# Second attention, heads without bias: the odd heads' weights are turned on VectorE, four weight low halves are made on GpSimd

## The reference

```python
s = jnp.einsum('bqhd,bkhd->bhqk', qb, k).astype(jnp.float32) * scale
s = jnp.where(key_idx[None, :] <= q_idx[:, None], s, NEG_INF)
p = jax.nn.softmax(s, axis=-1).astype(v.dtype)
return jnp.einsum('bhqk,bkhd->bqhd', p, v)
# second_block: a_out from mla_attention, b_out from moba_attention
x = x + jnp.concatenate([a_out, b_out], axis=-1) @ w_out[l]
```

## Time and profile before

| | us |
|---|---|
| median of three runs | 966.04 (965.82 to 966.35) |
| profiled execution | 966.08 |
| its span, first to last instruction | 964.2 |
| TensorE busy | 956.4 |
| VectorE busy | 772.1 |
| ScalarE busy | 500.9 |
| GpSimd busy | 162.5 |
| TensorE's granted clock | 0.999 of 2.4 GHz |

### The profile page before, as it was taken

How to read it: one execution, slowest core, us unless ns; L and a number is a source line. 1 busy time by engine, 2 the same in 40 slices (tenths; PEclk the granted TensorE clock), 3 DMA queues, 4 the chain that set the end, 5 groups by cost and what they waited for, 6 DMA issues and landing times.

```text
span 964.2 us, 12923 instructions
## 1 busy us (share of the span) xinstructions
PE 956.4 (99%) x4468; PEld 786.7 (82%) x4468; DVE 772.1 (80%) x1489; ACT 500.9 (52%) x666; POOL 162.5 (17%) x118
## 2 busy tenths in 40 slices
PE   9999999999999999999999999999999999999997
PEld 6887778888888888888888888888887788888886
DVE  6897997578669799884778987877878878887875
ACT  7545556644463644444765444444648665444442
POOL 3552444310013300000133000000133023000000
PEclk9999999999999999999999999999999999999999
DMA  9865555434455755554566656553654255656531
GB/s 343 269 193 167 165 174 175 150 130 175 175 203 205 240 176 191 202 187 164 172 215 196 213 177 204 187 177 113 223 182 147 88 175 187 206 177 206 184 131 44
DMA packets 98725, 175.67 MB, mean 182 GB/s; under 512 B 5920, under 2 KB 54128, under 8 KB 98672
## 3 DMA queue, kind: packets, MB, share of 16 engines
q1 hardware_dynamic: 97024, 171.53, 53.0%
q0 software_dynamic: 1344, 3.19, 1.2%
q10 hardware_dynamic: 304, 0.27, 0.1%
HBM read 173.91 MB, written 1.05 MB: 181 GB/s over the span
## 4 chain that ended last, share of the span: by engine, by line
PE 93%; DVE 4%; issue 1%; ACT 1%; POOL 1%; DMA 0%; POOLq 0%; ACTq 0%; DVEq 0%
PE bank L519 86%; PE bank L533 2%; DVE relu_T L1755 2%; DVE w_lo L1479 1%; PE bank L578 1%; PE bank L577 1%; PE bank L904 1%; PE bank L589 1%; POOL w_lo L2159 0%; ACT w_hi L1034 0%; PE bank L960 0%; DMA g_rows<-in_g_mix 0%; PE bank L591 0%; PE bank L590 0%; DVE act_f L1740 0%
## 5 line engine op out<-in xcount | busy, mean ns | idle before, releaser
L519 PE MATMUL bank<-w_hi,hA 128*128 128x512 f32 (+1 forms) x1752 | 544.8, 390 | 0.0
L1034 ACT ACTIVATE w_hi<-raw 128x2048 fp32r<-128x2048 f32 (+1 forms) x162 | 305.8, 1893 | 196.7 <-PE bank L519 194.9
L519 PEld LDWEIGHTS bank<-w_hi,hA 128*128 128x128 f32 x1752 | 327.4, 188 | 67.7 <-issue 1.1
L1479 DVE TENSOR_TENSOR w_lo<-raw,w_hi 128x2048 fp32r<-128x2048 f32 (+1 forms) x138 | 308.2, 2254 | 63.1 <-ACT w_hi L1034 58.1
L519 PE MATMUL bank<-w_lo,hA 128*128 128x512 f32 (+1 forms) x876 | 334.3, 388 | 0.0
L519 PEld LDWEIGHTS bank<-w_lo,hA 128*128 128x128 f32 x876 | 164.5, 188 | 33.0
L2159 POOL TENSOR_TENSOR w_lo<-raw,w_hi 128x2048 fp32r<-128x2048 f32 x21 | 96.8, 4609 | 154.5 <-ACT w_hi L1034 121.9
L1848 DVE STREAM_TRANSPOSE act_T<-act_f 32x128 f32<-32x128 f32 x352 | 106.5, 303 | 5.7 <-DVE act_f L1836 0.7
L2145 POOL TENSOR_SCALAR ms<-ss 128x1 f32<-128x1 f32 x15 | 9.8, 654 | 515.9 <-ACT junk L1064 515.6
L519 PE MATMUL bank<-w_hi,fT_hi 128*128 128x512 f32 x232 | 71.5, 389 | 0.0
L519 PE MATMUL bank<-w_hi,fT_lo 128*128 128x512 f32 x232 | 71.4, 389 | 0.0
(11 more groups left out here) (281 smaller groups left out, 906.7 us busy)
## 6 DMA issues: line engine op xcount, KB each, us to landing
raw<-in_w_in SPq DMA_DIRECT2D x74, 512.0 KB, 4.7
raw<-in_w_ff SPq DMA_DIRECT2D x64, 512.0 KB, 4.0
raw<-in_ffn_w_gate SPq DMA_DIRECT2D x44, 512.0 KB, 3.9
raw<-in_ffn_w_up SPq DMA_DIRECT2D x44, 512.0 KB, 4.8
raw<-in_ffn_w_down SPq DMA_DIRECT2D x44, 512.0 KB, 4.0
raw<-in_w_out SPq DMA_DIRECT2D x16, 512.0 KB, 3.8
raw<-in_w_branch_diff SPq DMA_DIRECT2D x8, 512.0 KB, 3.9
raw<-in_w_branch_ret SPq DMA_DIRECT2D x8, 512.0 KB, 3.7
```

Source lines behind the costliest of these rows:

```text
L519: mm = pe.matmul(o, a, w, start=first and t == 0 and m < len(outs), stop=last and t == n - 1 and m >= len(todo) - len(outs))
L1034: act.activation(w_hi[u % HI_SLOTS][:, 0:w], raw[u % RAW_SLOTS][:, 0:w], ACT.Copy).then_inc(hi_ready, 1)
L1479: vec.tensor_tensor(w_lo[u % RAW_SLOTS][:, 0:w], raw[u % RAW_SLOTS][:, 0:w], w_hi[u % HI_SLOTS][:, 0:w].bitcast(f32), ALU.subtract).then_i ...
```

## The change

For kind "l" the odd head of a pair is not transposed on TensorE any more and has no work batch. VectorE, after the logits of the next pair, transposes its normalised weights from `L` straight to `aT[1]` in sixteen instructions of 32 partitions and counts `odd_turned`; TensorE waits for that count ahead of the odd head's weighted sums. VectorE's copy from PSUM goes for these heads. The low halves of o2 + 1, o2 + 2, o2 + 3 and f2 are taken from VectorE and appended to GpSimd's list behind the last gain's load; VectorE waits for f2's before it makes that of f2 + 1. ScalarE's `cat_split` waits for the same two pairs as before, by names in place of batch numbers.

```diff
--- before.py
+++ after.py
@@ -116,7 +116,7 @@
     order += [("cq", 0), ("cq", 1), ("ckv",)]
     for kind in "bl":
         for j in range(BH // 2):
-            order += [(kind + "a", 2 * j), (kind + "a", 2 * j + 1)]
+            order += [(kind + "a", h) for h in range(2 * j, 2 * j + 2) if kind == "b" or h % 2 == 0]
             order += [(kind + "v", j)]
     order += [("ffn2", tb, h) for tb in range(TB) for h in range(2)]
     return {name: n for n, name in enumerate(order)}
@@ -348,7 +348,7 @@
     heads_out = [sem("heads_out0"), sem("heads_out1")]
     k_full = sem("k_full")
     a_turned = sem("a_turned")
-    m_turned = sem("m_turned")
+    m_turned, odd_turned = sem("m_turned"), sem("odd_turned")
     a_ready, cat_hi, cat_ready = sem("a_ready"), sem("cat_hi"), sem("cat_ready")
     vec_step, pool_step = sem("vec_step"), sem("pool_step")
     last_half, half_added, half_squared = sem("last_half"), sem("half_added"), sem("half_squared")
@@ -891,6 +891,8 @@
                     head_scores(kind, h)
             for h in (2 * j, 2 * j + 1):
                 m = SOFT[kind, h]
+                if kind == "l" and h % 2:
+                    continue
                 pe.wait_ge(a_ready, m - 2 * DH + 1)
                 turn((kind + "a", h), [L[:, m % 4, b * P:(b + 1) * P] for b in range(3)])
             beside()
@@ -898,7 +900,10 @@
             b = work(name)
             work_free(WB[name])
             for h in (2 * j, 2 * j + 1):
-                turned((kind + "a", h))
+                if kind == "l" and h % 2:
+                    pe.wait_ge(odd_turned, j + 1)
+                else:
+                    turned((kind + "a", h))
                 v = [mv[:, tb, h * BD:(h + 1) * BD] if kind == "b" else v_tm[:, tb, h, :] for tb in range(TB)]
                 a, y = aT[h % 2], b[h % 2 * BD:(h % 2 + 1) * BD]
                 pe.matmul(y[:, 0:SEQ], v[0], a[:, 0:SEQ], start=True, stop=False, skip_group_check=True)
@@ -1339,8 +1344,7 @@
 
         def cat_split(n):
 
-            b = WB[("l" if n < 2 else "b") + "v", 2 * (n % 2) + 1]
-            for k in (b - 3, b):
+            for k in (WB[("l" if n < 2 else "b") + "v", 2 * (n % 2) + j] for j in range(2)):
                 act.wait_ge(work_out[k % 2], k // 2 + 1)
             act.activation(hA[0][:, 2 * n:2 * n + 2, :], yT[:, 2 * n:2 * n + 2, :], ACT.Copy).then_inc(cat_hi, 1)
 
@@ -2016,6 +2020,15 @@
 
             if not last:
                 next_pair(kind, j + 1)
+            if kind == "l":
+                whole = L[:, SOFT["l", 2 * j + 1] % 4, :].rearrange("p (b j f) -> p b j f", j=4, f=32)
+                there = aT[1][:, :].rearrange("p (b a c) -> p b a c", a=4, c=32)
+                vec.wait_ge(a_ready, SOFT["l", 2 * j + 1] - 2 * DH + 1)
+                for a in range(4):
+                    for k in range(4):
+                        t = vec.transpose(there[32 * k:32 * k + 32, :, a, :], whole[32 * a:32 * a + 32, :, k, :])
+                t.then_inc(odd_turned, 1)
+                return
             n = WB[kind + "a", 2 * j + 1]
             vec.wait_ge(work_done, n + 1)
             vec.tensor_copy(aT[1][:, :], work((kind + "a", 2 * j + 1))[:, 0:384]).then_inc(work_out[n % 2], 1)
@@ -2095,24 +2108,19 @@
         cat_split(3)
         normalize_pair("l", 0)
         pair("l", 0, False)
-        lo(U0["o2"] + 1)
         normalize_pair("l", 1)
         pair_y("l", 0)
         pair("l", 1, False)
-        lo(U0["o2"] + 2)
         normalize_pair("l", 2)
         pair_y("l", 1)
         pair("l", 2, False)
         cat_split(0)
         normalize_pair("l", 3)
         pair_y("l", 2)
-        lo_half(U0["o2"] + 3, 0)
         pair("l", 3, True)
-        lo_half(U0["o2"] + 3, 1)
         pair_y("l", 3)
-        lo_half(U0["f2"], 0)
         cat_split(1)
-        lo_half(U0["f2"], 1)
+        vec.wait_ge(lo_ready, U0["f2"] + 1)
         lo(U0["f2"] + 1)
         x_add("o2", 0, 1.0)
         split_rows("ffn2", 0)
@@ -2252,6 +2260,8 @@
             block_bias(h)
         pool.wait_ge(c_src, 4)
         load_gain("final", g_final)
+        for u in (U0["o2"] + 1, U0["o2"] + 2, U0["o2"] + 3, U0["f2"]):
+            low(u)
         rstd("ffn2")
         for n in (5, 7):
             low(U0["f2"] + n)
```

## The result

The changed kernel takes 988.32 us (median of 5 runs, 987.78 to 989.55) against 966.04: slower, by a ratio of 1.0233 (95% interval 1.0222 to 1.0243). Its profiled execution took 989.55 us with a span of 987.7.

What follows compares the result with a forecast made beforehand. It took TensorE's gapless list as the bound, with VectorE overtaking it in the second attention. Turns 7.8 plus blocks 3.8, 3.4, 3.0 and 3.7, less 0.5, gave 21.2 us, so 987.3 us; 976 to 993 us held 0.8.

Steps and rivals of the forecast that it cites:

- the turns: Kind "l", VectorE: sixteen transposes per odd head take 4.55 us, making its round 7.60 us; +7.8 us in total.
- the four blocks: GpSimd low halves hold up VectorE in kind "b", pairs 1 and 2 of "l", and cat_split(0): +3.8, +3.4, +3.0, +3.7 us.
- the clock: Rival: TensorE's new waits put it at the lower clock level, adding +1 to +6 us, 988.3 to 993.3 us; chance 0.12.
- TensorE's list: Kind "l": 12 fewer transposes save 1.3 us, 0.33 per pair, leaving a round of 5.39 us.
- TensorE's waits: Kind "l": 1.9 us waits ahead of each odd head's weighted sums, released by VectorE's aT.
- the forecast's own sign: Pair 3 of kind "l": if its sums come without a wait, the turn is cheaper than its profile row.
- The choice between the ends of the sharing's cost: VectorE beside GpSimd: from 0.8 us in all up to the rest of a 4.6 us instruction each time; upper taken.
- Who is first in kind "b": At head 4's TENSOR_SCALAR, GpSimd or VectorE may start first; left open, about 4.25 or 4.1 us late, mattering little.
- the main case: Whole kernel: turns plus whole-instruction blocks, 987.3 us, within 983 to 992 us; chance 0.58.
- The other half of that rival: At the lower clock, output(2, 1) after the last wait would take 5.5 us instead of 2.75.
- Only a slowing: Rival: GpSimd merely slows VectorE's normalisations, 7.8 + 0.8 = 8.6 us, 974.7 us; chance 0.13.
- Faster: Rival: turns fit at 0.15 us a transpose, GpSimd is harmless, only TensorE's 1.3 us counts, 964.8 us; chance 0.02.

Runs made afterwards that it cites:

- four_turns: The changed kernel with low halves back on VectorE and four 128-partition transposes per odd head instead of sixteen (weights in wrong places): 965.32 us.
- beside_turns: The changed kernel with each of GpSimd's four low halves held back until VectorE starts a turn: 973.83 us.
- gpsimd_only: The kernel before the change with the four low halves on GpSimd, odd heads still transposed on TensorE: 972.19 us.
- first_beside: The changed kernel with only the first of GpSimd's low halves (o2+1) held back until head 1's turn: 984.04 us.
- keep_warm: The changed kernel with 13 unread matmuls filling TensorE's wait for head 4's normalised weights in kind "b": 987.01 us.
- same_quarter: The changed kernel with low halves back on VectorE and each odd head's sixteen transposes kept in their own partition quarter (weights in wrong places): 972.82 us.
- quarters: The changed kernel with each of GpSimd's four low halves cut into four instructions of 512 columns: 988.22 us.

## Why the prediction was right

The forecast was 987.3 us and the time 988.3: the turns, the four blocks and the path were as worked out. Without the clock the profiles show 21.1 us where the sum has 21.2. The clock, for which it had nothing, added 2.1 us in one profile and 1.5 in the other (23.2 and 22.6; 22.3 by the medians). That it added no more is luck: the two later falls lay where TensorE had to wait for VectorE anyway, the last with nothing to spare. Point by point:

- *TensorE's list.* The round of a pair with a cheap turn, in four_turns, is about 5.4 us as worked out. The gain there was 1.1 us in the profile, near the 1.3 worked out.
- *The turn.* 4.55 us from the earlier trace rows was 4.54 (755.26 to 759.80). The 7.8 us worked out from it are the 7.8 us of beside_turns, with two small errors that cancel: in beside_turns the last turn ends about 0.4 us earlier than drawn (775.4 against 775.8), and the odd head's sums behind a turn take 0.85 us and not about 0.4, as long as both heads' together in the earlier trace rows.
- *TensorE's waits.* They were expected at 1.9 us ahead of each odd head's sums. They are 1.29, 0.84 and 2.43 us in the changed kernel, and head 7's sums come without one (791.17). By the forecast's own sign that would mean a cheaper turn. It doesn't: that turn took 4.50 us, and TensorE, slowed by the clock from 785 us on, was ready only when it ended.
- *The choice between the ends of the sharing's cost.* The upper one held. Both rows on which it rested were short instructions caught near the end of GpSimd's work; they showed the rule, and the four blocks of 2.9 to 4.4 us its size. The four terms, 3.8, 3.4, 3.0 and 3.7, were 3.84, 3.45, 2.86 and 3.64. The turn of 146.41 that showed transposes to be untouched did not lie wholly beside its low half, which began 0.16 us later; beside_turns has the same overlap and the same 4.51 us. That copies and logits from PSUM are untouched was assumed, and gpsimd_only shows it.
- *Who is first in kind "b".* By the records VectorE's first TENSOR_SCALAR starts 0.05 us before GpSimd (734.12 against 734.17), yet it is the one that waits: taken singly it takes 4.63 us, and the second, from 738.68, its usual 0.34. As said, it made no difference to the sum. GpSimd slipping in between two TENSOR_SCALARs is what first_beside shows: the first takes 0.29 us from 753.46, the low half starts at 753.60, and the second, from 753.66, takes 4.60.
- *The clock.* This step was mis-sized: the sum had nothing for it, and it was a rival with a chance of 0.12 and a price of 1 to 6 us. It fell behind the block in kind "b" in every profile that has it but keep_warm's, and cost 1.3 to 2.1 us there. So this rival came true in part, beside the main case. The other half of that rival was wrong: output(2, 1) starts after 6.9 us of nearly unbroken work on TensorE and runs at full speed (0.72 us for its first two matmuls, as the 0.74 of the earlier trace rows).
- *The other rivals.* "Only a slowing" would have been 974.7; the lock's timelines exclude it. "Faster" would have needed 0.15 us a transpose; with 0.17 and four of them, in four_turns, the kernel did get there.

## What to carry to other kernels

Before work is moved to an idle GpSimd, look at what VectorE does at that time: in this kernel a pair of TENSOR_SCALARs of 0.55 us cost up to 4.35 us more, nearly the length of GpSimd's instruction, while stream transposes, reads from PSUM and the TENSOR_SCALAR with an accumulator output ran beside it without a wait. So place GpSimd's work beside those by a semaphore, or change the form, and don't count on shorter pieces. And an engine at 98% in a stretch has no room for a longer path even where its total over the program is 80%: sum its round, not its share.

## What the runs showed of the hardware that was not expected

A VectorE transpose of 32x96 starts 0.28 us after the one before it in the turn, where the output's partitions change every time, and mostly 0.16 us after it in same_quarter within a quarter (4.51 against 3.04 us for sixteen, the latter with three changes of partition, 0.24 us each). The Trainium skill ("VectorE: DVE Perf Modes", Two Vector instructions with no wait between them) says that an instruction with another start quadrant than the one before it starts only when that has finished; the two turns agree. A transpose of all 128 partitions was as quick as one of 32 (four in 0.75 us).

Where both wanted it, GpSimd and VectorE took turns after single instructions, also between two back-to-back instructions of the same engine: in first_beside GpSimd's low half of 753.60 got in between two TENSOR_SCALARs, and in quarters each TENSOR_SCALAR from 734.16 to 739.35 waited for a piece of its own. The start in the records doesn't tell who goes first: at 734.12 VectorE's instruction has the earlier one, and it waited.
